# Transposed probabilities of a sparse-attention kernel: one raw copy by ScalarE, its high part by VectorE and its low part by GpSimd

## The reference

```python
logits = jnp.einsum('bqngd,bqknd->bqngk', qg, kg.astype(jnp.float32)) * (HEAD_DIM ** -0.5)
logits = jnp.where(valid[:, :, None, None, :], logits, NEG)
p = jax.nn.softmax(logits, axis=-1)
o = jnp.einsum('bqngk,bqknd->bqngd', p, vg.astype(jnp.float32))
```

## Time and profile before

| | |
|---|---|
| median of 3 runs | 3897.79 us (3894.25 to 3903.45) |
| the profiled execution, its own time | 3904.1 us |
| its span | 3902.1 us |
| TensorE clock granted, mean | 0.898 |
| busy: PE, DVE, ACT, POOL | 79%, 54%, 42%, 32% of the span |
| the eight attention lots | 829 us, of which PE is busy 640 and POOL 83 |

### The profile page before, as it was taken

The page is one execution under the profiler, slowest core; times in us unless marked ns, Lnnn a source line. Parts: engine busy times, 40 slices in busy tenths (PEclk is TensorE's granted clock), DMA queues, the critical chain, the costliest instruction groups (busy, mean ns, idle before and its releaser), DMA issues.

```text
span 3902.1 us, 46669 instructions
## 1 busy us (share of the span) xinstructions
PE 3068.9 (79%) x14520; PEld 2365.7 (61%) x14520; DVE 2112.6 (54%) x4935; ACT 1643.6 (42%) x2887; POOL 1254.2 (32%) x1180
## 2 busy tenths in 40 slices
PE   7997537376578887796798778977888878879997
PEld 6886422134466666564577666645676666668886
DVE  4433953834457975558676554376784555431112
ACT  3322414513356744376463434655743434322222
POOL 1322621232014551153255012532672111324444
PEclk9998768677779998998899999988999999989999
DMA  4444354354335563254444223434343231444443
GB/s 152 132 138 142 85 152 103 106 183 137 100 131 213 213 220 111 99 197 154 151 174 165 66 91 104 147 107 178 144 178 113 68 109 48 161 184 160 153 173 116
DMA packets 227312, 542.43 MB, mean 139 GB/s; under 512 B 58858, under 2 KB 121388, under 8 KB 200924
## 3 DMA queue, kind: packets, MB, share of 16 engines
q1 hardware_dynamic: 215708, 516.86, 38.9%
q0 software_dynamic: 11360, 22.60, 1.9%
HBM read 411.23 MB, written 135.33 MB: 140 GB/s over the span
## 4 chain that ended last, share of the span: by engine, by line
PE 39%; DVE 14%; issue 9%; ACT 4%; POOL 4%; DMA 3%; SPq 0%; POOLq 0%; DVEq 0%; ACTq 0%
PE r L1679 16%; PE r L1711 11%; DVE pT_b L2433 3%; PE tr L1754 2%; DVE prob_b L2466 2%; POOL acc_b L2179 2%; ACT junk_a_b L2044 2%; PE sc L1727 1%; PE po L1765 1%; PE sc L1739 1%; PE sc L1740 1%; POOL hr_b L2160 1%; PE tr L1727 1%; DMA x_d<-acc_b 1%; PE r L1645 1%
## 5 line engine op out<-in xcount | busy, mean ns | idle before, releaser
L2179 POOL TENSOR_TENSOR acc_b<-acc_b,part_b 128x512 f32<-128x512 f32 x373 | 517.3, 1407 | 552.3 <-ACT part_b L1995 551.8
L1711 PE MATMUL r<-ready_b,h_b 128*128 128x512 f32 x2304 | 575.7, 406 | 56.7 <-ACT part_b L1995 46.9
L1711 PEld LDWEIGHTS r<-ready_b,h_b 128*128 128x128 f32 x2304 | 440.6, 195 | 180.2 <-ACT part_b L1995 58.9
L1679 PE MATMUL r<-x_hi_b,ready_b 128*128 128x512 f32 x1536 | 493.2, 394 | 5.4 <-DVE x_lo_b L2284 2.8
L2160 POOL TENSOR_TENSOR hr_b<-hr_b 128x512 f32<-128x512 f32 x128 | 151.5, 1184 | 880.0 <-ACT hr_b L1982 879.9
L2044 ACT ACTIVATE junk_a_b<-score_b,trial_b 128x384 int8<-128x384 f32 (+13 forms) x266 | 347.2, 1305 | 114.5 <-DVE trial_b L2370 113.7
L1679 PEld LDWEIGHTS r<-x_hi_b,ready_b 128*128 128x128 f32 x1536 | 291.4, 190 | 76.1 <-issue 10.1
L1995 ACT ACTIVATE part_b<-r 128x512 f32<-128x512 f32 x388 | 222.8, 594 | 238.6 <-PE r L1711 144.2
L2071 ACT ACTIVATE pT_b<-tr 128x512 fp32r<-128x512 f32 (+3 forms) x320 | 169.7, 530 | 336.2 <-PE tr L1754 335.8
L1679 PE MATMUL r<-x_lo_b,ready_b 128*128 128x512 f32 x768 | 301.5, 393 | 0.0
L1754 PE MATMUL tr<-ident_sb,prob_b 128*128 128x128 f32 x1088 | 188.1, 291 | 105.7 <-DVE pT_b L2433 87.2
(11 more groups left out here) (414 smaller groups left out, 6441.0 us busy)
## 6 DMA issues: line engine op xcount, KB each, us to landing
ready_b<-ws_u SPq DMA_DIRECT2D x96, 1024.0 KB, 6.9
ready_b<-ws_d SPq DMA_DIRECT2D x96, 1024.0 KB, 4.9
ws_u<-up_b SPq DMA_DIRECT2D x32, 1024.0 KB, 8.5
ws_d<-dn_b SPq DMA_DIRECT2D x30, 1024.0 KB, 6.4
kv_b<-kv_pages POOLq DMA_DIRECT2D x128, 128.0 KB, 3.4
kv_b<-kv_pages SPq DMA_DIRECT2D x128, 128.0 KB, 3.1
raw_b<-w_out SPq DMA_DIRECT2D x64, 256.0 KB, 3.5
raw_b<-w_up SPq DMA_DIRECT2D x32, 512.0 KB, 5.6
```

The lines of the kernel that those rows point to most:

```text
L1679: mm = pe.matmul(x[:], wt[:, c], y[:, k], start=k == n == 0, stop=(k, n) == (KD - 1, 2))
L1711: mm = pe.matmul(x[:], f[:, tok], w[:, col], start=c == n == 0, stop=(c, n) == (KQ - 1, 2))
L2179: pool.tensor_tensor(dst, dst, part[:, add_no[key] % 2, :], ALU.add).then_inc(add_pool, 1)
```

## The change

ACT copies the transposed bank as it is (f32) from PSUM into a new SBUF ring `raw_pT` of two slots. DVE makes the high part from that copy (a `tensor_copy` from f32 to fp32r, SBUF to SBUF). POOL makes the low part: it subtracts the high part from the copy. PE may refill a `tr` bank once ACT's copy has been made (`pT_raw_ok`). ACT's copy waits until POOL has finished with the slot (low part of bank j - 2); DVE's copy waits for its slot in `pT` (values of bank j - 3), for which ACT had waited. POOL takes the subtraction at the same unit as DVE had. `vsum` loses its second slot, so `sum_values` waits for the fold of the previous head in place of the one before it.

```diff
         pT = place_at("pT", [P, 3, 4, 2, P], F32R)
+        raw_pT = place_at("raw_pT", [P, 2, 4, P])
...
-        vsum = place_at("vsum", [P, 2, P])
+        vsum = place_at("vsum", [P, P])
...
-                        pe.wait_ge({"p": pT_lo_ok, "f": o_ok, "o": aT_ok}[kind], m + 1)
+                        pe.wait_ge({"p": pT_raw_ok, "f": o_ok, "o": aT_ok}[kind], m + 1)
...
                 def keep_prob(t, h, b):
                     i, j = turn_no["p", t, h, b], prob_no[t, h, b]
-                    wait(act, pT_used, j - 2)
                     m = min(4, t + 1 - 4 * b)
                     act.wait_ge(tr_full, i + 1)
-                    act.activation(pT[:, j % 3, 0:m, 0, :], tr[i % 2][:, 0:m * P].rearrange("p (k q) -> p k q", q=P),
-                                   ACT.Copy).then_inc(pT_hi_ok, 1)
+                    wait(act, pT_lo_ok, j - 1)
+                    act.activation(raw_pT[:, j % 2, 0:m], tr[i % 2][:, 0:m * P].rearrange("p (k q) -> p k q", q=P),
+                                   ACT.Copy).then_inc(pT_raw_ok, 1)
...
+                def low_prob(t, h, b):
+                    j, m = prob_no[t, h, b], min(4, t + 1 - 4 * b)
+                    hi, lo = pT[:, j % 3, 0:m, 0, :].bitcast(F32), pT[:, j % 3, 0:m, 1, :]
+                    pool.wait_ge(pT_hi_ok, j + 1)
+                    pool.tensor_tensor(lo, raw_pT[:, j % 2, 0:m], hi, ALU.subtract).then_inc(pT_lo_ok, 1)
+
                 for u in plan:
...
+                    elif u[0] == "A" and (u[1], u[2] - 1) in bank_of:
+                        low_prob(*bank_of[u[1], u[2] - 1])
...
-                def low_prob(t, h, b):
-                    n, j = turn_no["p", t, h, b], prob_no[t, h, b]
-                    m = min(4, t + 1 - 4 * b)
-                    dve.wait_ge(pT_hi_ok, j + 1)
-                    dve.tensor_tensor(pT[:, j % 3, 0:m, 1, :], tr[n % 2][:, 0:m * P].rearrange("p (k q) -> p k q", q=P),
-                                      pT[:, j % 3, 0:m, 0, :].bitcast(F32), ALU.subtract).then_inc(pT_lo_ok, 1)
+                def high_prob(t, h, b):
+                    j, m = prob_no[t, h, b], min(4, t + 1 - 4 * b)
+                    dve.wait_ge(pT_raw_ok, j + 1)
+                    wait(dve, pT_used, j - 2)
+                    dve.tensor_copy(pT[:, j % 3, 0:m, 0, :], raw_pT[:, j % 2, 0:m]).then_inc(pT_hi_ok, 1)
 
                 def sum_values(t, h):
                     n = head_no[t, h]
                     dve.wait_ge(pT_used, prob_no[t, h, banks(t) - 1] + 1)
-                    if n >= 2:
-                        dve.wait_ge(tr_full, turn_no["f", *head_at[n - 2]] + 1)
-                    c.step(dve.tensor_copy(vsum[:, n % 2, :], po[:, 0, 0:P]))
-                    dve.tensor_tensor(vsum[:, n % 2, :], po[:, 0, P:2 * P], vsum[:, n % 2, :], ALU.add).then_inc(vsum_ok, 1)
+                    if n:
+                        dve.wait_ge(tr_full, turn_no["f", *head_at[n - 1]] + 1)
+                    c.step(dve.tensor_copy(vsum[:], po[:, 0, 0:P]))
+                    dve.tensor_tensor(vsum[:], po[:, 0, P:2 * P], vsum[:], ALU.add).then_inc(vsum_ok, 1)
...
-                        low_prob(*bank_of[s, j - 1])
+                        high_prob(*bank_of[s, j - 1])
```

More of the change, by code:

```diff
@@ L1278, in blend @@
         q_ld, m_ld = [sem("q_ld0_"), sem("q_ld1_")], [sem("m_ld0_"), sem("m_ld1_")]
-        sc_full, sc_free, nmx_ok, prob_ok, tr_full, pT_hi_ok, pT_lo_ok, aT_ok, pT_used, mz_ok = (
-            sem(x) for x in ("sc_full", "sc_free", "nmx_ok", "prob_ok", "tr_full", "pT_hi_ok", "pT_lo_ok", "aT_ok", "pT_used", "mz_ok"))
+        sc_full, sc_free, nmx_ok, prob_ok, tr_full, pT_raw_ok, pT_hi_ok, pT_lo_ok, aT_ok, pT_used, mz_ok = (
+            sem(x) for x in ("sc_full", "sc_free", "nmx_ok", "prob_ok", "tr_full", "pT_raw_ok", "pT_hi_ok", "pT_lo_ok", "aT_ok", "pT_used", "mz_ok"))
         vsum_ok, o_ok, mz_st, ks_ld, v2_ld = (
@@ L1774, in fold_values @@
                     x = turn_bank(("f", t, h))
-                    pe.matmul(x[:, 0:HD], vsum[:, n % 2, :], halves_one[:], start=True, stop=True).then_inc(tr_full, 1)
+                    pe.matmul(x[:, 0:HD], vsum[:], halves_one[:], start=True, stop=True).then_inc(tr_full, 1)
                 def turn_output(t, v):
```

## The result

The changed kernel took 3780.21 us in the median (3775.98 to 3786.86, 4 runs); the kernel before, on the same chip, 3900.49 us (3894.25 to 3903.45, 4 runs). The ratio is 0.9695, with a 95% interval of 0.9676 to 0.9715: 120 us faster. The prediction was 3847 us, in a range of 3795 to 3900. The sign and the mechanism were right; the gain is more than twice the 51 us that the sum gave, and 15 us outside the range.

The account below looks back on a forecast made before the run. The prediction took PE's wait for a tr bank that DVE returns late as the bound in attention. Gains of 19, 19, 8 and 5 us made 51, taking 3897.8 us to 3847, in a range of 3795 to 3900.

Parts of the forecast that it names:

- What bounds the kernel: Attention's eight lots: PE idle about 190 us, mostly waiting for a tr bank that DVE gives back late.
- Why late: Shown lot 3 head: DVE's subtraction starts only at 1587.26, behind other DVE work, though ACT had copied at 1585.90.
- The sum: Gains per pair of lots: 2 banks 19 us, 3 banks 19, 4 banks 8, 1 bank 5; together 51.
- 2-bank head: Shown lot 3 head: 3.6 to 3.7 us in place of 4.55, gain 0.9; mean taken as 0.6.
- The 4-bank head: Shown lot 6 head, 7.97 us: exponential already ends the cycle; gain only one subtraction less one copy, 0.25 us.
- DVE's copy, POOL's subtraction: For 512 columns: DVE's copy 0.42 to 0.44 us against 0.68 for its subtraction; POOL's subtraction 1.30 us.
- The lock: A DVE operation meeting a running POOL operation stands until it ends; round trip 1.87 us for 512 columns.
- The new waits: ACT's copy waits for POOL two banks back, met or late by tenths; pT and single vsum slots cost nothing.
- Lots 0 and 1, page loads: POOL's subtractions stand behind page loads, up to 3.65 us late; gain 5 us taken, bounds gain 16, loss 10.
- Rival 1: The round trip becomes the pace, from about 2.1 us per 512-column bank: loss 36 us, 3934; chance 0.13.
- Rival 3: The wait only changes its name: heads end at an exponential starting no earlier; gain 0 to 7, 3894; chance 0.08.
- Rival 2: POOL's blocking of DVE is not felt, PE's wait nearly vanishes: gains 93 us and 10, 3795; chance 0.14.

Follow-up runs that it names:

- experiment 1: Changed kernel, but PE refills a tr bank only when POOL's low part is made; 4202.01 us, ratio 1.0768 to the kernel before.
- experiment 2: Changed kernel, but PE refills a tr bank only when DVE's high copy is made; 3881.67 us, ratio 0.9949 to the kernel before.
- experiment 5: Changed kernel, but ACT copies raw and then makes the high part, DVE subtracts from SBUF, POOL left out; 3771.87 us, ratio 0.9666 to the kernel before.
- Experiment 9: Kernel before, with only 36 of 320 banks freed early by ACT's raw copy, those with an output turn among the next two uses; 3868.74 us, ratio 0.9910.
- experiment 12: Kernel before, with 136 banks freed early by ACT's raw copy: 36 near an output turn, 100 before a fold and then the very next transposes; 3778.48 us.
- experiment 7: Changed kernel with one more POOL operation between its wait for the high part and each bank's subtraction; 3822.20 us, ratio 0.9789 to the kernel before.
- experiment 3: Changed kernel, but DVE makes both high and low part from ACT's raw copy, POOL does none of it; 3841.18 us, ratio 0.9849 to the kernel before.
- experiment 8: Changed kernel, but DVE does a head's last mask before the high copy instead of after it; 3826.87 us, ratio 0.9812 to the kernel before.
- experiment 4: Changed kernel, but ACT makes the high part, DVE copies the bank raw and so frees it, POOL subtracts; 3917.46 us, ratio 1.0041 to the kernel before.
- experiment 11: Kernel before, with only 184 of 320 banks freed early by ACT's raw copy: those neither near an output turn nor before fold and very next transposes; 3891.23 us.

## Why the prediction was wrong

**What bounds the kernel: right.** The bank that DVE gives back late holds PE. Experiments 1 and 2 (same work, later return: the gain gone) and 5 (same return, other division of work: the gain kept) show it.

**Why late: right.** In the earlier trace rows it was DVE's list and not its 0.68 us; over all banks 0.9 us of 1.5 is time in the list.

**The sum: this is the step that failed.** All four of its terms, the gains of heads with 1, 2, 3 and 4 banks, were too small: 5, 19, 19 and 8 us forecast, 26.7, 35.7, 34.7 and 32.2 measured. Three mistakes are behind it, and a term that was not there.

1. *The exponential was held fixed.* For the 2-bank head I let it stand at its old place, 2.39 us after the head's start, and got 3.6 to 3.7 us. But the masks ahead of it follow score matmuls and a DVE list that are in the same loop as the bank; it came at 2.00, and the next head at 3.19. A gain of 1.36 in the head where I had worked out 0.9.
2. *The 4-bank head.* "The exponential is what ends the cycle already" was a misreading of the earlier trace rows: between its end and the transposes lay 0.49 us, where a hop is 0.14. It had 0.35 of slack, and the late transposes of 3066.84 set the end. And "one subtraction less one copy" miscounts DVE's list: two subtractions lie between the head's first transposes and its last mask, worth 0.36 + 0.26. Together 0.97 in place of 0.25, and for the 32 heads 32 us in place of 8.
3. *The count.* I worked out single heads and then discounted them (0.9 to 0.6, with no row for the discount), took the 3-bank heads as a mean, bounded lots 0 and 1 by guesses, and never looked at the heads at an item's end, where the output turn shifts the order of the two banks. One 3-bank head there went from 7.05 to 4.94 us. Experiment 9 puts these places at 37 us alone; 69 us were missing in the sum. (The 136 banks of experiment 12 at the shown head's 0.9 would give 122 us, but that is hindsight: the order of the turns alone does not single them out from the 86 that a fold wants a step later, and 0.9 was itself too small for that head.)
4. *PE's busy time.* The sum took from PE's idle time alone. Of the 129 us that the lots lost, 103 are idle time and 26 busy time (641.7 to 615.9) for the same matmuls, at a granted clock of 0.75 to 0.98 in the lots before and 0.80 to 1.00 after. Busy time times clock, summed over the lots, gives 605 before and 601 after, so by this estimate some 22 of the 26 went with the clock. No experiment took it apart, and experiment 7 shows that busy time also grows at the same clock.

**DVE's copy, POOL's subtraction: right to 0.02 us for 512 columns**, 0.42 and 1.28 us at the median. The line through 128 and 1604 columns failed for 384: 0.54 us in place of 0.35. These 32 copies were slower than that, beside POOL or alone, and not blocked.

**The lock: there, but smaller.** A copy of 512 columns that meets a running POOL operation does wait for its end, but it is then done 0.28 us after it and not 0.42: POOL from 2960.86 to 2962.15, the copy from 2961.81 to 2962.43, and POOL's next 0.08 later. So it was with all 82 that met one with more than 0.15 us to go: they ended 0.280 to 0.288 us after it. The round trip is 1.28 + 0.28 + 0.08 = 1.64 us, not 1.87. In total the copies took 171.1 us, against 146.2 in experiment 3, where POOL has none of this work: 25 us. So 0.14 of the 0.42 us wasn't paid again behind POOL's end.

That such an operation stands until POOL's ends was read from the earlier trace rows for "a DVE operation of this kind", and the trace of the kernel before bears it out for both lines. Of the 17 copies on L333 16 met a POOL operation: they took 0.54 to 0.55 us and ended 0.08 to 0.09 us behind it; the one that met none took 0.22. Of the 64 splits of 1024 columns on L2265 22 met one that had more than 0.15 us to go: they took 1.31 to 2.33 us and ended 1.08 behind it; the others took 1.22 to 1.23. Of DVE operations in general it does not hold: the 23 subtractions of 512 columns on L2433, with one input in PSUM, that met a POOL operation with more than 0.10 us to go took 0.68 to 0.69 us, as did the 201 others, and the 384-column copies above did not stand for POOL either.

**The new waits: half right.** "Met or late by tenths" is 59 us for ACT's copies and 21 for PE's values in all (38 in their weight loads' row). Experiments 7 and 8 show that POOL's lateness is felt: a third of what was added to its list. It is a price inside the gain, as experiment 5, without POOL, is at least as fast. The single `vsum` slot was not tested by itself; experiments 2, 4 and 11 have it too, and with the bank returned late they gain 17, -19 and 15 us, so it does not bring the gain.

**Lots 0 and 1, page loads: right in that nothing was lost**; the 26.7 us were a term that I had set at 5 for fear of them.

**The rivals.** Rival 1, the round trip as the pace, did not come; 1.64 us lies well under its 2.1. Rival 3 was wrong in its condition: the exponential does start earlier. Rival 2 was the nearest (gains of 1.1, 1.0, 0.8 and 10 us for lots 0 and 1: 3795), and its three heads' gains were nearly those measured (1.1, 1.1, 1.0). I gave it 0.14 for the place of the exponential in the earlier trace rows, which is mistake 1 and 2 again.

What stays open: how much of PE's last waits in the changed kernel (exponential 27.6 us, sum of the values 35.9 us) could still be had, and how much of the gain is clock. A third slot for the raw copies wasn't tried.

## What to carry to other kernels

When a buffer is returned late, look first at the order in which its turns are taken, find the places where the same buffer is wanted again at once, and ask for each what would hold the engine next if the wait were gone; the total of a wait by name is not its price (kernel 12 kept 71 of the folds' 73 us and had the whole gain). Do not add a wait of PE and one of its weight loads: they can be one pause. Before you take another engine as next late, check that it leaves only a hop before its user, and that its own start does not hang on the wait that is removed. Here the copy out of PSUM by ACT is what paid, which was free when the transposes ended (1585.30 behind 1585.20 in the earlier trace rows); who did the arithmetic afterwards mattered by what it added to a full list. Which engine is faster at the operation did not decide: the subtraction took 1.28 us on POOL and 0.68 on DVE, and moving it beside DVE's full list (experiment 3) was 63 us slower than leaving it on POOL (57 us gained in place of 120). With the high part on ScalarE (experiment 5) VectorE had room for it, and the kernel was at least as fast as with POOL.

## What was unexpected of the hardware

- A DVE copy of 512 columns that was blocked by POOL ended 0.28 us after POOL's instruction both where it met a POOL subtraction (above) and where it met an addition: POOL 2087.34 to 2088.62, the copy 2087.80 to 2088.90. Alone it takes 0.42. For 256 columns it is 0.15 (alone 0.28), for 128 columns 0.08 (alone 0.22); with 384 columns, three blocks of 128, the copy took 0.54 us beside POOL or alone.
- A DVE subtraction with both inputs in SBUF took 0.68 us at the median (experiment 5), no more than with one input in PSUM.
- In experiment 1 PE stood more and its granted clock was lower: 0.854 over the span, where PE was idle for 329 of the lots' 1110.6 us, against 0.902 in the changed kernel, where it was idle for 83 of 698.7. In lot 7 it went from 0.97 to 1.00. The idle time alone does not order the kernels: experiment 7, with 88 us of it in the lots, had 0.897, the kernel before, with 186, 0.898.
